# Two transformer blocks on one core: the order of work in the sparse-attention stage is rewritten, with a second query buffer

## The reference

```python
q = rms_norm(parts[0].reshape(B, T, G, HG, DH), q_norm)          # 16 heads of 64
kc, vc, ksl, vsl, kw, vw = [a.reshape(B, T, G, DH) for a in parts[1:7]]   # 4 groups
gates = sigmoid(parts[7])                                        # 16 heads x 3 branches
k_cmp = rms_norm(compress(kc, pos_k, k_w1, k_b1, k_w2), kcmp_norm)   # 15 blocks of keys
v_cmp = compress(vc, pos_v, v_w1, v_b1, v_w2)    # gelu(block @ w1 + b1) @ w2
...
o = gb[..., 0:1] * o_c + gb[..., 1:2] * o_s + gb[..., 2:3] * o_w     # three branches
return o.reshape(B, T, NSA_HEADS * DH) @ w_out
```

## Time and profile before

| | us |
|---|---|
| median of 3 runs | 1194.47 (1193.97 to 1194.67) |
| the profiled execution | 1191.17 |
| its span, first to last instruction | 1189.3 |
| TensorE busy | 1138.2 |
| VectorE busy | 638.3 |
| ScalarE busy | 579.0 |
| GpSimd busy | 170.4 |
| mean granted clock of TensorE | 0.981 |

### The profile page before, as it was taken

How to read it: one execution, slowest core, us unless ns; L and a number is a source line. 1 busy time by engine, 2 the same in 40 slices (tenths; PEclk the granted TensorE clock), 3 DMA queues, 4 the chain that set the end, 5 groups by cost and what they waited for, 6 DMA issues and landing times.

```text
span 1189.3 us, 16109 instructions
## 1 busy us (share of the span) xinstructions
PE 1138.2 (96%) x6875; PEld 996.0 (84%) x6875; DVE 638.3 (54%) x643; ACT 579.0 (49%) x861; POOL 170.4 (14%) x224
## 2 busy tenths in 40 slices
PE   6999999999999999998789999999999899999998
PEld 5777888888999888875578889999888678999987
DVE  5543544466554454564555556555356556555543
ACT  5687554444455443545245344434347654544431
POOL 1022201110322000321450000000006600000000
PEclk9999999999999999999897899999999899999999
DMA  9533443454655555523030044544534304454542
GB/s 344 211 107 131 152 142 127 157 177 174 208 189 186 195 192 184 202 106 142 34 144 1 1 178 163 192 177 177 191 137 160 151 26 162 169 199 172 195 164 84
DMA packets 28103, 184.40 MB, mean 155 GB/s; under 512 B 3312, under 2 KB 3568, under 8 KB 7792
## 3 DMA queue, kind: packets, MB, share of 16 engines
q1 hardware_dynamic: 26496, 177.52, 41.7%
q0 software_dynamic: 1536, 5.86, 1.5%
HBM read 182.31 MB, written 1.05 MB: 154 GB/s over the span
## 4 chain that ended last, share of the span: by engine, by line
PE 86%; DVE 5%; ACT 5%; POOL 2%; issue 2%; DMA 1%; SPq 0%; POOLq 0%; ACTq 0%; DVEq 0%
PE ps L528 14%; PE ps L530 14%; PE ps L531 14%; PE ps L557 9%; PE ps L559 9%; PE ps L558 9%; PE ps L509 5%; PE ps L638 4%; PE ps L618 3%; ACT t L1094 3%; DVE t L1629 3%; POOL t L2218 2%; ACT t L1091 1%; PE ps L855 1%; DMA t<-in_w 1%
## 5 line engine op out<-in xcount | busy, mean ns | idle before, releaser
L1629 DVE TENSOR_TENSOR t<-t 128x2048 fp32r<-128x2048 f32 (+6 forms) x281 | 430.6, 1543 | 340.4 <-ACT t L1094 330.7
L1094 ACT ACTIVATE t<-t 128x2048 fp32r<-128x2048 f32 (+5 forms) x224 | 331.8, 1502 | 238.3 <-PE ps L531 135.9
L528 PE MATMUL ps<-t 128*128 128x512 f32 (+2 forms) x834 | 328.0, 393 | 4.0 <-DVE t L1629 2.1
L530 PE MATMUL ps<-t 128*128 128x512 f32 (+2 forms) x834 | 323.5, 388 | 0.7 <-DVE t L1629 0.7
L531 PE MATMUL ps<-t 128*128 128x512 f32 (+2 forms) x834 | 323.6, 388 | 0.0
L557 PE MATMUL ps<-t 128*128 128x256 f32 x960 | 272.1, 283 | 0.7 <-DVE t L1629 0.7
L559 PE MATMUL ps<-t 128*128 128x256 f32 x960 | 271.7, 283 | 0.0
L558 PE MATMUL ps<-t 128*128 128x256 f32 x960 | 271.7, 283 | 0.0
L528 PEld LDWEIGHTS ps<-t 128*128 128x128 f32 x834 | 157.1, 188 | 35.2 <-DVE t L1629 4.8
L557 PEld LDWEIGHTS ps<-t 128*128 128x128 f32 x960 | 184.3, 192 | 1.2 <-DVE t L1629 1.1
L558 PEld LDWEIGHTS ps<-t 128*128 128x128 f32 x960 | 184.3, 192 | 0.1
(11 more groups left out here) (94 smaller groups left out, 583.5 us busy)
## 6 DMA issues: line engine op xcount, KB each, us to landing
t<-in_w SPq DMA_DIRECT2D x158, 1024.0 KB, 4.8
t<-in_w SPq DMA_DIRECT2D x8, 512.0 KB, 3.5
t<-in_w SPq DMA_DIRECT2D x5, 768.0 KB, 4.2
t<-in_g POOLq DMA_DIRECT2D x6, 512.0 KB, 5.0
t<-in_w SPq DMA_DIRECT2D x2, 640.0 KB, 3.9
t<-in_x SPq DMA_DIRECT2D x4, 256.0 KB, 5.8
t<-in_mem POOLq DMA_DIRECT2D x1, 1024.0 KB, 10.4
out<-t SPq DMA_DIRECT2D x4, 256.0 KB, 4.0
```

The source lines that it names most:

```text
L528: e.matmul(o, sh, wh, start=k0 + j == 0, stop=False)
L530: e.matmul(o, sh, wl, start=False, stop=False)
L1094: return e.activation(o, src, ACT.Copy, scale=scale)
L1629: return e.tensor_tensor(o, a, b, op)
```

## The change

- The chunks come in another order: the first column block of `nsa` now holds the queries of heads 0 to 7, and the source of the compression (`nsc`) comes after the keys; the gates come before it.
- Queries of the second eight heads have a buffer of their own (`qA[1]`, `qB[1]`; two more DMAs on GpSimd's queue fill the latter's last rows). Before, they went into the one buffer once the first eight were through.
- The turned blocks (`turn_dup`), the products of the last query chunk (82, 83), of the compression (84 to 87), and half of a few turns move into the attention steps 0 to 15. Scores begin right after chunk 81, before any compression product.
- The units have another order: all main units but two first, the few units in steps 22 to 31. All steps use two score banks, 6 and 7. Values of a unit that opens an output bank come one step later (`late_opens`).
- Factors for both halves are made in one go (`head_factors`). The layout of the blocks moves from VectorE to GpSimd (`blocks`, four instructions in place of sixteen). The branches 1 and 2 of a group are joined together.
- GpSimd cuts chunk 91 too, and its four cuts follow each other behind step 21. Products of chunks 88 and 89 begin in steps 30 to 34, by halves.
- ScalarE and VectorE finish the first half of `nwo` (squares, add and gain) before they cut chunk 92.

The core of the diff:

```diff
-    ("nsa", 8, [512, 512, 512]), ("nsq0", 8, [512]), ("ngate", 8, [48]), ("cmpk", 16, [256]),
-    ("nsq1", 8, [512]), ("cmpv", 16, [256]),
+    ("nsa", 8, [512, 512, 512]), ("ngate", 8, [48]), ("nsc", 8, [512]), ("nsq1", 8, [512]),
+    ("cmpk", 16, [256]), ("cmpv", 16, [256]),
...
-POOL_CUTS = {("nwo", 0, 0), ("nwo", 0, 4), ("nwo", 1, 0)}
+POOL_CUTS = {("nwo", 0, 0), ("nwo", 0, 4), ("nwo", 1, 0), ("nwo", 1, 4)}
...
-        self.qA, self.qB = sb(N, [128, 8, T], F32R), sb(N, [72, 8, T], F32R)
+        self.qA, self.qB = [sb(N, [128, 8, T], F32R)], [sb(N, [72, 8, T], F32R)]
+        self.qA.append(sb(N, [128, 8, T], F32R))
+        self.qB.append([x[0:72, 0:4, :].rearrange("p a (b t) -> p (a b) t", t=128) for x in self.HT])
...
-    units = a + b[:7] + [e[0], e[1], b[7]] + [*f, *c]
-    units += [d[0], g[0], d[1], g[1], d[2], z[0], d[3], z[1], *d[4:]]
+    units = a + b + c + d[:6] + [*e, d[6], *f, d[7], *g, *z]
...
+TURNED_BY_ACT = range(2, 27, 3)
 NSA, NSA_GROUPS = nsa_units()
 MLA, MLA_GROUPS = mla_units()
-S_BANKS = {"fox": lambda i: (6, 7)[i % 2], "nsa": lambda i: (6, 7, 1)[i % 3] if i >= 14 else (6, 7)[i % 2],
-           "mla": lambda i: (6, 7, 0)[i % 3]}
-O_BANKS = {"fox": (2, 3), "nsa": (2, 3, 2, 3, 0, 2, 3, 0, 2, 3, 0, 0), "mla": (2, 3)}
+S_BANKS = {"fox": lambda i: (6, 7)[i % 2], "nsa": lambda i: (6, 7)[i % 2], "mla": lambda i: (6, 7, 0)[i % 3]}
+O_BANKS = {"fox": (2, 3), "nsa": (2, 3, 2, 3, 2, 3, 2, 3, 1, 1, 1, 1), "mla": (2, 3)}
...
-    turn_dup()
+    turn_queries(0, 0, 0)
     gemm(78, x, ready)
-    turn_keys(1)
-    gemm(79, x, ready)
-    gemm(80, x, ready)
-    turn_keys(2)
-    thin(81, 2, "n")
-    hidden(0, 82, range(8))
-    for h in range(2):
-        turn_queries(0, h, 0)
-    hidden(0, 83, range(8))
-    for h in range(2):
-        turn_queries(0, h, 1)
+    turn_queries(0, 0, 1)
+    thin(79, 1, "n")
+    gemm(80, x, ready, (0,))
+    turn_keys(1, 0)
+    gemm(80, x, ready, (1,))
+    turn_gates()
+    gemm(81, x, ready, (0,))
+    turn_keys(2, 0)
+    gemm(81, x, ready, (1,))
...
+    late_opens = [u.i + 4 for u in NSA[4:] if u.kind == "main" and u.opens]
     for i in range(35):
         if i < 32:
             nsa_scores(NSA[i])
+        if i in late_opens:
+            nsa_values(NSA[i - 4])
         if 2 <= i < 34:
             turn_rows(NSA[i - 2], m.P1)
-        if i >= 3:
+        if i in (1, 2):
+            turn_dup(i - 1, 0)
+            turn_dup(i - 1, 1)
+        if i < 3:
+            gemm(82 + i // 2, x, ready, (i % 2,))
+        elif i < 5:
+            gemm(83, x, ready, (1,), range(2 * i - 6, 2 * i - 4))
+        elif 8 <= i < 12:
+            hidden(0, 84 + (i - 8) // 2, range(4 * (i % 2), 4 + 4 * (i % 2)))
+        elif 12 <= i < 16:
+            hidden(1, 86 + (i - 12) // 2, range(4 * (i % 2), 4 + 4 * (i % 2)))
+        elif i in (30, 32):
+            gemm(88, lo_out, ready_out, (0,), range(i - 30, i - 28))
+        if i >= 3 and i + 1 not in late_opens:
             nsa_values(NSA[i - 3])
-        if i == 1:
-            gemm(84, x, ready, (0,))
-        elif i == 2:
-            gemm(84, x, ready, (1,))
+        if i < 2:
+            turn_keys(i + 1, 1)
+        elif i < 4:
+            turn_queries(0, 1, i - 2)
+        elif 9 <= i < 13:
+            turn_queries(1, (i - 9) // 2, (i - 9) % 2)
+        elif i == 14:
             turn_hidden(0)
-        elif i == 3:
-            gemm(85, x, ready, (0,))
-        elif i == 4:
+        elif i == 16:
             compressed(0)
-            gemm(85, x, ready, (1,))
+        elif i == 20:
             w.wait_ge(*after("keys copied"))
             turn(("kst",), [m.kst[:]])
-            w.wait_ge(*after("off", "ngate"))
-            for h in range(2):
-                turn(("ng", h), [m.ngt[:, half(h)]])
-        elif i in (6, 7, 8, 9):
-            hidden(1, 86 + (i - 6) // 2, range(4 * (i % 2), 4 * (i % 2) + 4))
-        elif i == 12:
+        elif i == 21:
             turn_hidden(1)
-        elif i == 13:
+        elif i == 22:
             compressed(1)
-        elif i in (14, 15, 18, 19):
-            turn_queries(1, (i - 14) // 4, i % 2)
-        elif i in (17, 20, 27):
-            turn_out(*{17: (0, 0), 20: (0, 1), 27: (1, 0)}[i])
-        elif i == 31:
-            gemm(88, lo_out, ready_out)
-    gemm(89, lo_out, ready_out, (0,))
+        elif i in (28, 31):
+            turn_out(0, (i - 28) // 3)
+        if i == 33:
+            gemm(89, lo_out, ready_out, (0,))
+            turn_out(1, 0)
+        elif i == 34:
+            gemm(88, lo_out, ready_out, (1,))
+    gemm(90, lo_out, ready_out, (0,))
     turn_out(1, 1)
     gemm(89, lo_out, ready_out, (1,))
-    gemm(90, lo_out, ready_out)
+    gemm(90, lo_out, ready_out, (1,))
...
-    cut(91)
     split(("no", 1, 1), m.HT[0][:, 4:8, half(1)])
+    squares_of_x("nwo", 0)
     cut(92)
-    squares_of_x("nwo", 0)
     cut(93)
...
+        if br:
+            f = m.cols("f", hg, h, n=16)
+            w.wait_ge(*after("on", "o", *g))
+            e.reciprocal(f, m.cols("sums", hg, h)).then_inc(*out(("over", hg, h)))
+            w.wait_ge(*after("over", hg, h))
+            tt(heads(f, 8), heads(f, 8), gates[:, 1:3], ALU.mult).then_inc(*out(("gated", hg, h)))
+            w.wait_ge(*after("gated", hg, h))
+            for i, o in ((1, dst), (2, tmp)):
+                tt(heads(o, 64), heads(bank("o", hg, h, i)[:, :], 64), bc(f[:, i * 8 - 8:i * 8], 64), ALU.mult).then_inc(
+                    *out(("off", "o", hg, h, i)))
+            w.wait_ge(*after("off", "o", hg, h, 2))
+        else:
+            divide(g, 8, 64, tmp, gates[:, 0])
+            w.wait_ge(*after("off", "o", *g))
+        tt(dst, dst, tmp, ALU.add).then_inc(*out(("joined", hg, h, 1 if br else 2)))
+        added[hg] = hg, h, 1 if br else 2
...
     split(("no", 1, 1), both(m.HT, 4, 8, 1))
+    add_and_gain("nwo", 0, "f1", G_FF0, lambda b, h: ("no", b, h))
     cut(92)
-    add_and_gain("nwo", 0, "f1", G_FF0, lambda b, h: ("n", b, h))
     cut(93)
     split_normed("f1", 0)
-    add_and_gain("nwo", 1, "f1", G_FF0, lambda b, h: ("n", b, h))
+    add_and_gain("nwo", 1, "f1", G_FF0, lambda b, h: ("no", b, h))
...
+    blocks(0)
+    blocks(1)
+    head_factors("nsq1", 0, 8, 1.0, 64 * EPS, "down")
+    w.wait_ge(*after("used", 83))
+    for h in range(2):
+        src = p_d[:, 0:2048].rearrange("p (n t) -> p n t", t=T)[:, :, half(h)]
+        e.dma_start(m.qB[1][h][64:72], src.bitcast(F32R)).then_inc(*places[3 + h](("places", 3 + h)))
...
+    cubic(1)
     ss = m.cols("ss cmp", n=1)[0:60]
     w.wait_ge(*after("mean cmp"))
     tt(ss, ss, m.half[0:60, 0:1], ALU.pow).then_inc(*out(("rms cmp",)))
     w.wait_ge(*after("off", "cmp", 0))
     e.tensor_copy(m.kst[:, 64:128], m.kst[:, 0:64]).then_inc(*out(("keys copied",)))
+    gelu(1)
     w.wait_ge(*after("stacked", "kst"))
     for g in range(2):
         t = e.tensor_copy(m.cB[0:64, g, :], m.cA[0:64].bitcast(F32))
         t.then_inc(*out(("copy of keys", g), *([("copied",)] if g else [])))
-    for h in range(2):
-        head_factor(("nsq1", 0, h), 8, 1.0, 64 * EPS, "down")
     cut(88)
-    cubic(1)
-    gelu(1)
     cut(89)
     cut(90)
+    cut(91)
```

402 lines of the change are left out of this document (224 added, 178 removed).

## The result

| | before | after |
|---|---|---|
| median, us | 1194.22 (4 runs, 1191.80 to 1194.67) | 1175.25 (4 runs, 1174.94 to 1176.38) |
| the profiled execution, us | 1191.17 | 1174.94 |
| mean granted clock | 0.981 | 0.982 |

The ratio is 0.9847 (95%: 0.983 to 0.9864), so the change takes 19.0 us off. The forecast was 25.5 off, 1169.0; the time lies inside the range of 1160 to 1185, 6.3 us above the forecast. Two executions stand far outside the others of their kernel, 2847.23 us in experiment 1 and 1197.05 in experiment 10, and the ratios leave them out.

What follows compares the result with a forecast made beforehand. TensorE was taken to bound the kernel. Its 148.2 us of work plus waits and clock loss summed to 163.1 us against 188.6, 25.5 less; with 3.30 carried over to the median, 1169.0 us, range 1160 to 1185.

Steps and rivals of the forecast that it cites:

- two hits: Kernel before: VectorE products with two SBUF operands held by GpSimd subtractions, costing 8.2 and 10.8 us with the half clock.
- Head, steps 0 to 4 and 8 to 15: Start of the stage and its filled attention steps: 0.5 us of waiting up to step 0, none in the other steps.
- Steps 5 to 8: Attention steps: VectorE's surplus 1.5 us and late hand-overs 1.4 make 2.9 us of waiting, bounds 1 and 5.
- Steps 16 to 22: Unfilled attention steps: late joins and the compressed keys bring 0.8 us of waiting.
- Step 33: Late attention step: waits 0.8 us for an output bank that the join of the step before frees.
- Way out: End of the stage: two cuts ahead of VectorE's split make the feed-forward wait 2.9 us, bounds 0.7 and 3.7.
- One fall, 5 us; bounds 0 and 15: Unfilled steps 16 to 29, a stretch of 31 us: TensorE's clock falls once, for 10 us, costing 5 us.
- the prediction's own sign: Clock reading is right if 1.00 up to step 16 with one fall after; wrong if under 0.8 over steps 16 to 29.
- the forecast's own narrower range: 1163 to 1176 for the forecast case, with steps 5 to 8, way out and one partial hit at their bounds; chance 0.62.
- this rival: Clock stays low in the unfilled steps: half their work at half clock costs 15 us instead of 5, 1179; chance 0.18.
- GpSimd's cuts: Cuts of chunks 88 to 90 after step 21 barely meet VectorE's joins in steps 26 to 32: 2 us, bounds 0 and 9.5.
- the sign of being wrong that was named: Prediction is wrong if VectorE's small products again take 3 us beside a GpSimd subtraction.

Runs made afterwards that it cites:

- experiment 1: Changed kernel with ScalarE and VectorE cutting chunk 92 before the squares, adds and gains of the first half of `nwo`, as before the change: 1176.03 us.
- experiment 10: Kernel before, with two GpSimd waits for VectorE's joins, ahead of cutting chunks 88 and 90: 1177.25 us.
- Experiment 6: Changed kernel with one cut in place of two ahead of the feed-forward's first split; chunk 93 is cut later: 1171.39 us.
- experiment 2: Changed kernel with four extra products of 512 columns, read by nobody, in each of steps 17 to 29: 1177.10 us.
- experiment 4: Changed kernel with the compression's products bunched as whole chunks in steps 8 to 11, leaving steps 12 to 29 unfilled: 1186.61 us.
- experiment 9: Changed kernel with GpSimd waiting for the first few group's join before cutting chunk 90, and one cut instead of two ahead of the feed-forward's first split: 1164.86 us.
- experiment 12: Unchanged repeat of the changed kernel with both GpSimd's wait before chunk 90 and one cut ahead of the feed-forward's first split: 1164.92 us.
- Experiment 5: Changed kernel with one added wait: GpSimd waits for VectorE's join of the first few group before cutting chunk 90: 1163.72 us.
- experiment 7: Changed kernel with four extra products of 512 columns a step, read by nobody, in steps 22 to 29 only: 1170.22 us.

## Why the prediction came out as it did

*The frame was right.* The stretch, its split into work, idle and clock, and the two causes of before: work 147.3 (148.2 forecast), idle 8.8 (9.9), and two hits worth 19 by the prediction and 17.3 by experiment 10.

*Head, steps 0 to 4 and 8 to 15:* no gap over 0.5 us in any of them, where the sum had 0.5. *Steps 5 to 8:* 0.82 + 0.58 and a third of 0.38, 1.8 in all, where 2.9 was set; the longest is behind ScalarE, not the gap of 1 to 3 us behind VectorE's join that was named as the sign. *Steps 16 to 22:* 0.48 + 0.36 (0.8). *Step 33:* 0.74 (0.8). *Way out:* 2.83 (2.9), behind the split, with two cuts ahead, just as worked out. It had a second price that the term lacked: the clock was low for 3.4 us behind it, which is why more than 1 us moved outside the stretch. Experiment 6 puts both together at 3.9. *Missed:* 1.42 us at 657, TensorE waiting for the last split of the heads.

*The clock is the step that failed.* "One fall, 5 us; bounds 0 and 15" was 14.6 in the profile, one fall of 24 us and two of 3.4. By the prediction's own sign its clock reading is wrong, if barely: under 0.8 over steps 16 to 29, and 0.79 was measured. The rest of the sum made up 2.1 of those 9.6, and outside the stretch 0.4 and 1.35 were added: 9.3 above the forecast for the profiled execution, 6.3 between the medians. The median even lies in the forecast's own narrower range of 1163 to 1176, but that was built from other terms: the clock alone would have brought 1179, and what brought it back was smaller waits and luck, a median 0.3 us above its profiled execution where 3.3 were carried over. 

The prediction took the length of one fall before, 10 us, for that of the next. That fall ended at 660.6, and the one ahead of it at 633, both in steps without fill and with no denser work begun. TensorE before, four turns on either side of that end:

```profile
658.72 1.06 PE L509 MATMUL ps<-t 128*128 128x128 f32 x4
...
660.54 0.60 PE L509 MATMUL ps<-t 128*128 128x128 f32 x4
```

The new one ended at 640.4, 3.4 us after the output products had begun. Why it didn't end sooner isn't shown. One thing that changed there is the order of the units, and no run tests it: from 616 to 637 now stand four few units and one main unit, where from 650 to 661 there were one few and two main units. The prediction put 0.18 on this rival, at 1179. Its price of 15 is what the profile has, though only some 9 of it are lost in steps 16 to 29 and the rest behind them, up to 661.

The rule cited there, of the Trainium skill, "TensorE: Matmul & The Clock Gate", section Part 4, that transpose-mode work doesn't count as busy, would have given 15. The trace and experiments 2 and 4 agree with it, but can't tell the turns from the small matmuls beside them; and in the profiles of experiments 9 and 12 the same steps 16 to 29 ran at 1.00 throughout, which the rule doesn't explain.

*GpSimd's cuts were placed wrongly.* "the first two meet the last half microsecond of a subtraction, the others none. I take 2" was the reading. The join of step 26 met the third subtraction 0.75 us after its beginning and was held for 4.33; the placing was off by some 3 us, as much as it was said to be good to. So the sign of being wrong that was named, VectorE at 3 us beside a GpSimd subtraction, came true in an add of 4.33. Experiment 5 prices it at 11.5 us between medians, over the bound of 9.5, and experiments 6, 9 and 12 at 6.5. This isn't a second loss beside the 14.6: in the profiled execution of the changed kernel the hit itself cost at most the gap of 0.61, as the clock had fallen 5 us before. Where there is neither hit nor fall at 616, the prediction's 5 for the clock is about right (6.8 us at half in the stretch in experiments 9 and 12, 3.4 lost).

*What the change is worth.* The kernel before without its hits takes 1177.25, the changed one without its own 1163.72: the new order brings 13.5 us (11 by the two ratios). Between the kernels as they stand 19.0 are seen, since one removed two hits and brought another.

*Left open:* what starts the fall at 616 in some executions, when TensorE had had no gap over 0.36 us since 606; why it lasts; and whether the second layer's falls make up all of the upper group of experiments 9 and 12. Spreading two score banks back to three wasn't tried, as bank 1 holds outputs of the few units.

## What to carry to other kernels

Before a large reordering, look for single VectorE instructions that end together with a long GpSimd one; here a wait of one line per hit, that puts GpSimd's elementwise work behind the join, was worth 6 to 12 us each. When waits are taken out, ask what the clock does in the stretches that are then full of small matmuls, and see whether some dense work can stand there: extra products that nobody reads nearly paid for themselves (experiment 2) or more than that (experiment 7). And read the mean clock of every execution before two medians are compared: here it explains a spread of 1%.
